# Loading x and the first weights in alternating pieces, and moving two groups of small jobs, in a three-layer kernel

## The reference, cut to what matters

```python
h = rms_norm(x, norm_g)                      # y = x * rsqrt(mean(x*x) + eps) * g
(nq, nkc, nvc, nks, nvs, nkw, nvw, ng, ...) = split(h @ w_in)
kc = nsa_compress(rot(nkc), ...)             # rot: rotary embedding by cos, sin of positions
vc = nsa_compress(heads(nvc), ...)
gates = sigmoid(ng + gate_b)
a_out = nsa_attention(rot(nq), kc, vc, rot(nks), nvs, rot(nkw), nvw, gates)
...
# third layer
aq, ak, av, gq, gk, gv, ... = split(a @ w_in_2)
y_att = windowed_gqa(partial_rope(aq), partial_rope(ak), av, sink) @ w_branch_attn
```

## Time and profile before

| what | value |
|---|---|
| median of 3 runs | 2427.57 us |
| the profiled execution's own time | 2427.69 us |
| its span | 2425.8 us |
| TensorE busy | 2277.8 us (94%) |
| VectorE busy | 663.2 us (27%) |
| ScalarE busy | 485.7 us (20%) |
| mean granted TensorE clock | 0.974 |
| transfers | 317.34 MB, mean 131 GB/s |

### The profile page before, as it was taken

The page is one execution under the profiler, slowest core; times in us unless marked ns, Lnnn a source line. Parts: engine busy times, 40 slices in busy tenths (PEclk is TensorE's granted clock), DMA queues, the critical chain, the costliest instruction groups (busy, mean ns, idle before and its releaser), DMA issues. The chain is left out here.

```text
span 2425.8 us, 19949 instructions
## 1 busy us (share of the span) xinstructions
PE 2277.8 (94%) x8258; PEld 1096.0 (45%) x8258; DVE 663.2 (27%) x1160; ACT 485.7 (20%) x982; POOL 0.2 (0%) x4
## 2 busy tenths in 40 slices
PE   6999999999999998889989999998978899999897
PEld 3644555544444445434534455553454333333343
DVE  3154544413200113531144244431131010101124
ACT  2223334310001013211113324322021000000022
POOL 0000000000000000000000000000000000000000
PEclk9899999999999999999999999998989999999998
DMA  5411112122211120012212212121424999999930
GB/s 156 81 55 50 35 36 70 44 78 74 99 70 69 70 66 22 5 45 73 55 69 70 70 35 70 35 62 52 173 104 190 409 409 409 409 409 409 409 149 35
DMA packets 156714, 317.34 MB, mean 131 GB/s; under 512 B 38960, under 2 KB 65712, under 8 KB 156624
## 3 DMA queue, kind: packets, MB, share of 16 engines
q1 hardware_dynamic: 144624, 309.64, 34.9%
q10 hardware_dynamic: 12000, 6.42, 1.1%
HBM read 313.95 MB, written 2.10 MB: 130 GB/s over the span
## 5 line engine op out<-in xcount | busy, mean ns | idle before, releaser
L350 PE MATMUL bank<-hT,ring 128*128 128x512 f32 (+1 forms) x1776 | 795.8, 601 | 34.5 <-DMA ring<-in_l_w_in 21.3
L350 PEld LDWEIGHTS bank<-hT,ring 128*128 128x128 f32 (+1 forms) x1776 | 329.0, 190 | 430.7 <-issue 406.8
L2049 PE MATMUL bank<-ring,xg 128*64 128x512 f32 x896 | 228.8, 601 | 15.7 <-DMA ring<-in_w_exp_gate 10.4
L350 PE MATMUL bank<-ring,hT 128*128 128x512 f32 (+2 forms) x704 | 230.8, 487 | 3.6 <-ACT proj L409 3.6
L350 PEld LDWEIGHTS bank<-ring,hT 128*128 128x128 f32 x704 | 117.8, 200 | 107.3 <-issue 103.5
L2049 PEld LDWEIGHTS bank<-ring,xg 128*64 128x64 f32 x896 | 73.0, 139 | 162.8 <-issue 161.7
L350 PE MATMUL bank<-rz,ring 128*128 128x512 f32 x256 | 113.7, 603 | 10.2 <-PEq L1312 10.2
L2082 PE MATMUL bank<-ring,hidT 128*64 128x512 f32 x384 | 113.3, 595 | 8.9 <-ACT hidT L2125 4.9
L350 PEld LDWEIGHTS bank<-rz,ring 128*128 128x128 f32 x256 | 49.5, 194 | 73.2 <-issue 73.2
L2082 PEld LDWEIGHTS bank<-ring,hidT 128*64 128x64 f32 x384 | 34.9, 137 | 77.6 <-issue 69.9
L350 PE MATMUL bank<-proj,ring 128*128 128x512 f32 x160 | 68.9, 592 | 1.1 <-PEq L1030 1.1
(11 more groups left out here) (413 smaller groups left out, 2153.9 us busy)
## 6 DMA issues: line engine op xcount, KB each, us to landing
ring<-in_w_exp_gate SPq DMA_DIRECT2D x32, 2048.0 KB, 17.0
ring<-in_w_exp_up SPq DMA_DIRECT2D x24, 2048.0 KB, 17.1
ring<-in_w_exp_down SPq DMA_DIRECT2D x24, 2048.0 KB, 18.4
ring<-in_l_w_in SPq DMA_DIRECT2D x19, 2048.0 KB, 7.8
ring<-in_w_in SPq DMA_DIRECT2D x10, 2048.0 KB, 7.8
hT<-in_w_exp_up SPq DMA_DIRECT2D x8, 2048.0 KB, 17.9
hT<-in_w_exp_down SPq DMA_DIRECT2D x8, 2048.0 KB, 23.1
ring<-in_l_w_out SPq DMA_DIRECT2D x8, 1152.0 KB, 6.1
```

The costliest lines, as they stand in the source:

```text
L350: mm = pe.matmul(self.out(n), *mats[i], start=i == 0, stop=i == len(mats) - 1)
L2049: mm = pe.matmul(bank[2 * which + n][e * 64:(e + 1) * 64, :], xg[p // 2 % 2][:, k, s:s + CAP], block_ap(j)[:, i, n * 512:(n + 1) * 512], s ...
```

## The change

First layer, loads: x comes in five pieces (of 1, 1, 2, 2 and 2 tiles), each followed on SyncE's queue by the same rows of kv1, which has a semaphore for each piece. Behind them on the same queue come cst, pos, kv2, memT and the 12 compression loads. ScalarE's queue keeps vec alone. First layer, work: ScalarE makes hT ahead of the square. TensorE does NKC, NKS and NVC side by side, step k of each before step k+1 (`abreast=3`), in three banks. NVC is evacuated behind the row job. The rotary arguments move on VectorE from the opening to behind NVC's evacuation, the sines on ScalarE to behind the last nvw tile, and the multiplication by the row is two operations of their own. The rotations of NKC and NKS come behind the nvw tiles, the copies of `shifts` with them, and `memory_act` goes behind the last gate tile. Third layer: the five rotations come before the four value tiles.

```diff
@@ squares_of
             def on_act(act, m):
+                act.activation(h[:, m, :], x[:, m, :], ACT.Copy, scale=gain(m)).then_inc(raw_ready, 1)
                 for i, g in enumerate(gains):
                     act.activation(sq[i][m], x[:, m, :], ACT.Square, scale=g(m)).then_inc(squared, 1)
-                act.activation(h[:, m, :], x[:, m, :], ACT.Copy, scale=gain(m)).then_inc(raw_ready, 1)
@@ run_products
-                    for n in range(len(jobs)):
+                    for k in range(KD):
+                        for n in range(abreast):
+                            dense.product(pe, n, k, k + 1)
+                    for n in range(abreast, len(jobs)):
                         dense.product(pe, n)
@@ opening
+        pieces = [(0, 1), (1, 2), (2, 4), (4, 6), (6, 8)]
...
         def load_x(sp):
-            for c in range(4):
-                sp.dma_start(xT[:, 2 * c:2 * c + 2, :], a["xT"][2 * c * P:(2 * c + 2) * P, :]
-                             .rearrange("(k p) n -> p k n", p=P)).then_inc(x_loaded[c], 16)
+            w0, dst = stream[0][0], block_ap(0)
+            for i, (lo, hi) in enumerate(pieces):
+                sp.dma_start(xT[:, lo:hi, :], a["xT"][lo * P:hi * P, :].rearrange("(k p) n -> p k n", p=P))\
+                  .then_inc(x_loaded[i], 16)
+                sp.dma_start(dst[:, lo:hi, :], w0[:, lo:hi, :]).then_inc(first_loaded[i], 16)
+            sp.dma_start(cst[:, :], a["consts"]).then_inc(cst_loaded, 16)
+            sp.dma_start(pos[:, :, :], a["pos"]).then_inc(pos_loaded, 16)
+            issue_blocks(sp, 2)
+            sp.dma_start(memT[:, :, :], a["memT"].rearrange("(k p) n -> p k n", p=P)).then_inc(memory_loaded, 16)
+            for i, kv in enumerate("kv"):
...
+        def turn_dve(dve, done):
+            dve.wait_ge(*done)
             dve.wait_ge(pos_loaded, 16)
             turns["dve"](dve)
+            dve.wait_ge(*turns["done"])
+            for x in (cos, sin):
+                dveq(dve.tensor_tensor(x, x, row, ALU.mult))
+            dveq.wait(dve)
@@ jobs of the first layer
         jobs[0]["ready"] = raw["ready"]
+        jobs[0]["rows"] = [(first_loaded[i], 16) for i in piece_of]
+        turn.append((NKS, fm(j, 256, NKS)))
+        fm_row(j, 128, NVC)
         cols = len(jobs)
         jobs.append(xfac.columns_job(xdiag, [raw["summed"], (cst_loaded, 16)]))
-        turn.append((NKS, fm(j, 256, NKS)))
-        jobs.append(xfac.row_job(xdiag, 0, cols, more=(cos, sin)))
-        jobs[cols]["dve_then"] = lambda dve, done: dve.wait_ge(*turns["done"])
-        fm_row(j, 128, NVC)
-        for t in range(TT):
-            tm(j, 384, 128, nvs[:, t, :], t)
-        jobs[-1]["act_then"] = load_compress
-        flush()
-        jobs[-2]["act_then"] = shifts(0)
-        jobs[-1]["act_then"] = shifts(1)
+        tm(j, 384, 128, nvs[:, 0, :], 0)
+        tm(j, 384, 128, nvs[:, 1, :], 1)
+        jobs[cols - 1]["late"] = len(jobs)
+        jobs[cols - 1]["dve_then"] = turn_dve
+        jobs.append(xfac.row_job(xdiag, 0, cols))
+        tm(j, 384, 128, nvs[:, 2, :], 2)
+        tm(j, 384, 128, nvs[:, 3, :], 3)
         j = EVEN["kv2"]
         turn.append((NKW, fm(j, 0, NKW)))
         for t in range(TT):
             tm(j, 128, 128, nvw[:, t, :], t)
-        jobs[-1]["act_then"] = memory_act
+        jobs[-1]["act_then"] = turn_act
+        for x in turn[:2]:
+            rotary(*x)
+        jobs[-2]["act_then"] = shifts(0)
+        jobs[-1]["act_then"] = shifts(1)
+        del turn[:2]
         for t in range(TT):
             jobs.append(dict(block=j, mats=tm_mats(j, 256, 24, hT, t), ..., eng="dve", evac=gate_evac(t)))
+        jobs[-1]["act_then"] = memory_act
         flush()
@@ jobs of the third layer
+        for i in range(4):
+            rotary2(AQ[i], c[i])
+        rotary2(AK, c[4])
         for t in range(TT):
             jobs.append(dict(block=W2["akv"], mats=tm_mats(W2["akv"], 128, 128, hT, t), ...))
-        for i in range(4):
-            rotary2(AQ[i], c[i])
-        rotary2(AK, c[4])
```

More of the change, by code:

```diff
@@ L172, in build @@
         w_loaded = [sem(f"w_loaded{i}") for i in range(WIDE)]
+        first_loaded = [sem(f"first_loaded{i}") for i in range(5)]
         tiles_done = sem("tiles_done")
@@ L283, in build @@
         for j in range(len(stream)):
-            level[slot(j)] += 16 * (1 if j not in special else 3 if j in WO0 else 16 if j in paired else 2)
+            level[slot(j)] += 16 * (0 if j == 0 else 1 if j not in special else 3 if j in WO0 else 16 if j in paired else 2)
             loads_of[j] = level[slot(j)]
@@ L295, in issue_blocks @@
                     load_special(sp, j)
-                else:
+                elif j > 0:
                     sp.dma_start(block_ap(j), stream[j][0]).then_inc(w_loaded[slot(j)], 16)
@@ L300, in wait_block @@
         def wait_block(pe, j):
-            pe.wait_ge(w_loaded[slot(j)], loads_of[j])
+            if j > 0:
+                pe.wait_ge(w_loaded[slot(j)], loads_of[j])
         class Jobs:
@@ L347, in product @@
                             pe.wait_ge(*job["ready"][i])
+                        if "rows" in job:
+                            pe.wait_ge(*job["rows"][i])
                         if "mats_after" in job:
@@ L369, in take, with run_products @@
                     job[kind + "_then"](eng, self.done_at[n])
-        def run_products(jobs, begin=None, upto=None, end_sync=None):
+        def run_products(jobs, begin=None, upto=None, end_sync=None, abreast=0):
             dense = Jobs(jobs, range(6))
@@ L684, in attention @@
             att["g"] += len(groups)
-        x_loaded = [sem(f"x_loaded{i}") for i in range(4)]
+        pieces = [(0, 1), (1, 2), (2, 4), (4, 6), (6, 8)]
+        x_loaded = [sem(f"x_loaded{i}") for i in range(len(pieces))]
+        piece_of = [i for i, (lo, hi) in enumerate(pieces) for _ in range(lo, hi)]
         vec_loaded, pos_loaded, cst_loaded = sem("vec_loaded"), sem("pos_loaded"), sem("cst_loaded")
@@ L713, in build @@
         mraw = squares_of(memT, [lambda m: 1.0], memh, lambda m: par("g_mem", m), [msq], mfac.accs)
-        turns = turns_of(pos[:, 0, :], con("inv"), *tiles("turn", range(60, 63)))
+        turns = turns_of(pos[:, 0, :], con("inv"), *tiles("turn", range(12, 15)))
         def load_x(sp):
-            for c in range(4):
-                sp.dma_start(xT[:, 2 * c:2 * c + 2, :], a["xT"][2 * c * P:(2 * c + 2) * P, :]
-                             .rearrange("(k p) n -> p k n", p=P)).then_inc(x_loaded[c], 16)
+            w0, dst = stream[0][0], block_ap(0)
[8 more added lines that the diff above has]
+            for i, kv in enumerate("kv"):
+                for g in range(2):
+                    for half in range(2):
+                        sp.dma_start(w1[g * 64:(g + 1) * 64, i, :, half, :], a[f"l0_cmp_w1_{kv}"]
+                                     [16 * half:16 * half + 16].rearrange("l d e -> d l e")).then_inc(cmp_loaded, 16)
+                    sp.dma_start(w2[g * 64:(g + 1) * 64, i], a[f"l0_cmp_w2_{kv}"]).then_inc(cmp_loaded, 16)
         def begin_act(act):
             act.dma_start(vec[:, :], a["vecs"]).then_inc(vec_loaded, 16)
-            act.dma_start(cst[:, :], a["consts"]).then_inc(cst_loaded, 16)
-            act.dma_start(pos[:, :, :], a["pos"]).then_inc(pos_loaded, 16)
-            act.dma_start(memT[:, :, :], a["memT"].rearrange("(k p) n -> p k n", p=P)).then_inc(memory_loaded, 16)
             act.wait_ge(vec_loaded, 16)
             for m in range(KD):
-                act.wait_ge(x_loaded[m // 2], 16)
+                act.wait_ge(x_loaded[piece_of[m]], 16)
                 raw["act"](act, m)
-            turns["act"](act)
         def begin_dve(dve):
@@ L737, in begin_dve, with turn_act @@
             dve.wait_ge(cst_loaded, 16)
+        def turn_dve(dve, done):
+            dve.wait_ge(*done)
             dve.wait_ge(pos_loaded, 16)
             turns["dve"](dve)
[L741 to L747, removed]
+            dve.wait_ge(*turns["done"])
+            for x in (cos, sin):
+                dveq(dve.tensor_tensor(x, x, row, ALU.mult))
+            dveq.wait(dve)
+        def turn_act(act, done):
+            turns["act"](act)
         def memory_act(act, done):
@@ L912, in build @@
         flush()
-        run_products(jobs, begin=dict(sync=load_x, act=begin_act, dve=begin_dve))
+        run_products(jobs, begin=dict(sync=load_x, act=begin_act, dve=begin_dve), abreast=3)
         units = []
```

## The result

The changed kernel takes 2403.35 us (median of 4 runs, 2401.28 to 2403.52); the kernel before took 2428.9 us beside it (4 runs, 2426.45 to 2430.62). The ratio is 0.9894, with a 95% interval of 0.9876 to 0.9911: about 25.6 us faster, where 29.1 were forecast. The time lies in the forecast's range, 4.9 us above the 2398.5 that was forecast.

What follows compares the result with a forecast made beforehand. The prediction took TensorE's waits as the bound: 21.3 us for the first weights, then the meeting at a block's end. Gains of 14.3 + 3.5 + 3.3 + 8.0 = 29.1 us from 2427.6 gave 2398.5 us, range 2391 to 2409.

Steps and rivals of the forecast that it cites:

- Start: First layer's opening: TensorE's start moves from 21.3 to 7.0 us, when hT[0] and kv1's first piece are there; 14.3 us gained.
- The bound of 10.8: Lower bound of the start's gain: a weights' piece takes 9.2 us from its issue, so TensorE starts at 10.5.
- No hole up to NQ0: First layer: TensorE's 3.56 us hole goes since ScalarE no longer issues 12 loads; 3.5 us gained.
- Clock in the opening: First layer: the clock falls about 5 us into the gates, losing 4.4 of the former 7.7 us; 3.3 us gained.
- Rival B: First layer: the clock holds through the gates, 4.4 us more gained, 2394.1 us; chance 0.18.
- Third layer: Third layer's opening: TensorE goes on 6.5 us sooner and its first product there saves 1.5 us at full clock; 8.0 us.
- Later stages hang on TensorE's progress, so they shift as a whole: Everything behind the changed openings: it moves earlier as a whole, with no further gain or loss counted.
- Rival D: Third layer: its gain doesn't come since SyncE or ScalarE holds the meeting at the block's end; 2406.5 us, chance 0.06.
- Narrow groups: After each group of narrow matmuls the clock may fall differently than before: 1.8 us either way.
- rival E: First layer: nq's transfers wait on SyncE's queue behind the 12 loads, TensorE waits at NQ0; slower, 2433 us, chance 0.03.
- Rival C: First layer: pieces come late, TensorE starts at 10.5 or waits between steps; 3.5 us less gained, 2402 us, chance 0.12.

Runs made afterwards that it cites:

- loads_on_scalar: The changed kernel with the 12 compression loads issued by ScalarE again, behind the last nvs tile: 2410.14 us, ratio 0.9920 to the kernel before.
- gates_128: The changed kernel with each gate matmul 128 moving columns wide in place of 24, only the last 24 used: 2398.31 us, ratio 0.9872 to the kernel before.
- later_1: The changed kernel with one extra, overwritten step at the start of the first product behind the third layer's opening: 2401.57 us, ratio 0.9886 to the kernel before.
- later_2: The changed kernel with two extra, overwritten steps at the start of the first product behind the third layer's opening: 2403.51 us, ratio 0.9893 to the kernel before.
- gates_later: The changed kernel with both the 128-column gate matmuls of gates_128 and the one extra step of later_1: 2397.27 us, ratio 0.9869 to the kernel before.
- same_again: The changed kernel itself, unaltered, measured a second time beside other runs on one chip: 2403.41 us, ratio 0.9891 to the kernel before.

## Why the prediction was right, and where it was off

**Start (14.3; measured 15.3).** The hT[0] chain was the limit, as said; the smaller piece of x landed 1.35 us sooner, where 0.3 was allowed. The bound of 10.8, slow pieces, was far off. But the first matmuls went slowly for longer (6 of them fill the first 5.3 us, where in the kernel before 9 fit into 5.0; the granted clock reads 1.00 over both, so what slows them stays open), so the three products took 23.1 us, and the columns job began at 29.16, where 29.2 follows from the forecast's terms.

**No hole up to NQ0 (3.5).** Right. `loads_on_scalar` shows the cause: with the loads back on ScalarE a hole of 3.2 us and 6.7 us of time come back, the clock's fall behind it included.

**Clock in the opening (3.3).** Right in mechanism, and nearly in size: the fall came 5.0 us into the gates, and it cost 1.9 us in the gates, 1.0 in the rotation and 0.5 in NQ0, 3.4 in place of 4.4. NQ0 ended at 72.12, where the forecast's terms give 73.0. `gates_128` shows that the columns cause it. Rival B, the clock holds, is refuted for the changed kernel.

**Third layer (8.0; 7.9 in its stretch, 5.6 in the kernel's time).** The stretch came out as worked out. The step that failed is "Later stages hang on TensorE's progress, so they shift as a whole". They don't. With the third layer's hole the clock's fall at that hole went too, and some 160 us later the clock now falls behind a short narrow stretch where it held before. That took back 1.7 of the 2.2 us (12.26 against 10.57). One extra step of 0.86 us in between undid it (`later_1`, `later_2`, `gates_later`). Rival D, that the gain of 8.0 doesn't come since something else holds the meeting, is refuted: 5.6 came, and nothing else held it.

**Narrow groups ("1.8 us either way").** The term was under-sized. In the first trace the stretch with the two groups behind NQ0 and NQ1 cost 5.0 us more than before, and 2.9 came back up to the third layer, in the retention; `same_again` had 0.0 and -0.1 there and lost 1.5 more up to NQ0's end, and the two spans differ by 0.4. Which early loss is paid back where is an account of single traces. That the totals of these two hardly follow them is shown. That the forecast's total came out within 3.5 us owes something to luck: the 2.9 us that came back were in none of its terms, and without them it would have been 6.4 off.

**The rest.** The transfers moved to SyncE's queue were hidden, VectorE's sines held nobody, and nq was no bound: rival E did not come. Rival C, late pieces, is refuted by the start at 6.02. The remaining -1.5 us in the last 780 lie in two places, both in the clock. The router's 64 matmuls of 16 columns with the products behind them take 19.14 us from 1764.91 at a granted clock of 0.55, where the kernel before took 18.05 from 1790.58 at 0.62. The products on rows_tm further on take 16.88 us at 0.87 in place of 16.32 at 0.90. No run tests what moved the clock there.

## What to carry to other kernels

At a kernel's start, the first product should need only the first piece of each operand. Load both in pieces in the order of use on one queue, and do several products step by step side by side if a single one would outrun the pieces (here 9.0 us of start for the weights' pieces, 2 us for the order). At the end of a block, put work that only TensorE and an idle engine share behind the work with the long evacuation. And before counting a saving as carried to the end, look at the granted clock behind each short, narrow stretch after it: here 0.86 us of work, put between the last low stretch of the clock and such a stretch, decided over 1.7 us.

## What the runs showed of the hardware that was not expected

Matmuls of 24 columns brought TensorE's clock from 1.00 to 0.50 with the engine never idle, and 128-column ones in the same place did not, so that five times the columns took 7.14 us in place of 9.04. Eight narrow matmuls between each pair of wide ones took 1.62 us a step where the same work in two separate groups took 1.33. And a short stretch with a hole of 0.95 us was followed by full clock or by 3.4 us of half clock. It fell in the nine traces in which it came 332.8 to 333.3 us behind the last low stretch, and held in the three in which a step of 0.86 us or two had been added in between (334.1 to 334.7), at whatever time of the execution it came.
